# A fused diffusion-backbone step: routing weight at eviction, expert pairs summed by the gather, outputs accumulated onto rows that hold the bias

## What is computed

```
def _layer_norm(x, g, b):
    y = (x - mean(x)) * rsqrt(var(x) + LN_EPS)
    return y * g + b

def _hier_moe(u, ...):
    p_group = softmax(u @ w_r1 + b_r1);  g_val, g_idx = top_k(p_group, 1)
    e_val, e_idx = top_k(fine logits of that group, 2)
    e_w = softmax(e_val) * g_val                  # two weights per token
    y = sum over the 2 experts of e_w * (silu(a) * b) @ w_down   # a, b = u @ w_up[expert]

x = _layer_norm(ALPHA * x + gate2 * _hier_moe(u2), ln2_g, ln2_b)
```

## Time and profile before

| | |
|---|---|
| runs of the kernel before | 1146.58, 1149.21, 1150.54 us (median 1149.21) |
| the profiled execution | 1147.15 us, of which the span is 1145.3 us |
| busy share of the span | PE 88%, PE weight loads 66%, DVE 54%, ACT 38%, POOL 15% |
| mean granted TensorE clock | 0.939 of 2.4 GHz |
| chain that ended last | PE 77%, DVE 12%, DMA 5%, ACT 3% |

### The profile page before, as it was taken

The page is one execution under the profiler, slowest core; times in us unless marked ns, Lnnn a source line. Parts: engine busy times, 40 slices in busy tenths (PEclk is TensorE's granted clock), DMA queues, the critical chain, the costliest instruction groups (busy, mean ns, idle before and its releaser), DMA issues.

```text
span 1145.3 us, 13287 instructions
## 1 busy us (share of the span) xinstructions
PE 1004.3 (88%) x4607; PEld 758.4 (66%) x4607; DVE 621.7 (54%) x897; ACT 438.1 (38%) x603; POOL 174.0 (15%) x139
## 2 busy tenths in 40 slices
PE   5899899998999999989998995389999999999800
PEld 1113799985777777766666774378888888888700
DVE  0176641100453455640317856676889965799548
ACT  0001422213343434421205002165787854788422
POOL 2035023000000000000000734111101101010056
PEclk9999999999999999999999896599999999999965
DMA  9995722204020302261207006487799997699552
GB/s 323 394 353 209 282 75 74 74 0 164 20 74 1 111 1 74 22 210 45 73 1 275 19 37 220 163 301 289 277 398 400 398 359 275 225 399 400 191 214 92
DMA packets 90747, 215.04 MB, mean 188 GB/s; under 512 B 6538, under 2 KB 7744, under 8 KB 90704
## 3 DMA queue, kind: packets, MB, share of 16 engines
q1 hardware_dynamic: 73904, 165.86, 40.1%
q10 hardware_dynamic: 11108, 30.07, 7.2%
q0 software_dynamic: 5696, 18.58, 4.6%
HBM read 191.37 MB, written 23.12 MB: 187 GB/s over the span
## 4 chain that ended last, share of the span: by engine, by line
PE 77%; DVE 12%; DMA 5%; ACT 3%; issue 2%; SPq 1%; ACTq 0%; POOL 0%; POOLq 0%; DVEq 0%
PE ps L1734 27%; PE ps L1521 22%; PE ps L1440 10%; PE ps L1507 7%; DMA ring<-in_w_mod 3%; PE ps L1625 2%; PE ps L1726 1%; PE ps L1492 1%; PE ps L1564 1%; DVE R_x L991 1%; DMA out<-small 1%; ACT w_hi L695 1%; PE ps L1619 1%; PE ps L1614 1%; PE ps L1761 1%
## 5 line engine op out<-in xcount | busy, mean ns | idle before, releaser
L1521 PE MATMUL ps<-w_hi,uT_hi 128*128 128x512 f32 x320 | 132.9, 415 | 7.2 <-ACT R_x L773 2.5
L1052 DVE TENSOR_TENSOR w_lo<-ring,w_hi 128x1024 fp32r<-128x1024 f32 x52 | 62.3, 1223 | 128.3 <-ACT w_hi L695 127.0
L1521 PE MATMUL ps<-w_lo,uT_hi 128*128 128x512 f32 x320 | 126.3, 395 | 0.0
L1440 PE MATMUL ps<-ring,small 128*2 128x512 f32 x192 | 87.6, 618 | 13.1 <-DMA ring<-in_w_mod 12.8
L1251 DVE TENSOR_TENSOR wa_lo<-ring,wa_hi 128x1024 fp32r<-128x1024 f32 x64 | 74.1, 1219 | 4.4 <-ACT wa_hi L851 4.0
L1521 PEld LDWEIGHTS ps<-w_hi,uT_hi 128*128 128x128 f32 x320 | 60.6, 189 | 23.7 <-issue 4.0
L1440 PEld LDWEIGHTS ps<-ring,small 128*2 128x2 f32 x192 | 16.5, 87 | 83.4 <-issue 82.2
L615 POOL TENSOR_TENSOR R_u<-R_m 128x1024 f32<-128x1024 f32 x1 | 2.4, 2397 | 449.6 <-DVE R_m L1218 449.6
L1521 PEld LDWEIGHTS ps<-w_lo,uT_hi 128*128 128x128 f32 x320 | 60.7, 190 | 13.4
L1734 PE MATMUL ps<-wa_hi,xgT_hi 128*128 128x512 f32 x152 | 62.9, 414 | 5.2 <-DVE xgT_lo L1358 5.2
L1521 PE MATMUL ps<-w_hi,uT_lo_a 128*128 128x512 f32 x160 | 64.0, 400 | 0.0
(11 more groups left out here) (345 smaller groups left out, 2238.1 us busy)
## 6 DMA issues: line engine op xcount, KB each, us to landing
ring<-in_w_up SPq DMA_DIRECT2D x64, 512.0 KB, 8.7
ring<-in_w_mod SPq DMA_DIRECT2D x12, 2048.0 KB, 18.0
ring<-in_w_in SPq DMA_DIRECT2D x11, 2048.0 KB, 7.9
R_d<-in_w_up SPq DMA_DIRECT2D x32, 512.0 KB, 10.9
R_p<-in_w_down SPq DMA_DIRECT2D x32, 512.0 KB
R_h<-in_w_down SPq DMA_DIRECT2D x32, 512.0 KB
y_slots<-R_m ACTq DMA_DIRECT2D x19, 512.0 KB, 6.3
R_s<-in_w_up SPq DMA_DIRECT2D x16, 512.0 KB
```

The source lines that it names most:

```text
L1052: tt(lo[:, at], weights(name)[:, at], hi[:, at].bitcast(F32), ALU.subtract).then_inc(S["w_split"], 1)
L1440: i = mm(out, lhs(k), rhs(k), start=(k == 0), stop=(k == n - 1))
L1521: i = mm(out, parts(k)[a][:, tok(j)], w[b][:, k], start=(k == 0 and a + b == 0), stop=(k == KD - 1 and b == 1))
```

## The change

Four edits. First, the weight of every slot is worked out in the routing: `hot_tile` times the token number goes to a table of its own (`hot_tok`), `hot_tile` times the weight stays in its place, and PE multiplies that with `hot_place` too (a second product, "wslot", into bank 0). DVE copies the result to `w_slot`. ACT's eviction copies the tile's column to `w_now` and scales by it, so that the stored rows are weighted already. Second, the gathers: both choices of block 0 and the first choices of blocks 1 to 4 are plain; the second choices of blocks 1 to 4 add themselves to the rows of the first (`compute_op=ALU.add`), each issued after its first choice has landed. ACT's scaling and DVE's weighted sum go away; DVE adds plainly for block 0. Third, `finish` now does (x - mean) * g2 over the whole block in one DVE instruction, and ACT multiplies by one over the deviation. Fourth, POOL writes `ln2_b` to all output rows near the start (five DMAs of 512 KB, DRAM to DRAM), and at the end it issues the five output stores as accumulating DMAs onto these rows. POOL's and DVE's products with `g2` and sums with `b2` go away.

```diff
@@ routing, DVE and PE
-                i = tt(hot, hot, const("tok").rearrange("p (j a) -> p j a", a=1).to_broadcast([P, NT, MAXT]), ALU.mult)
+                i = tt(hot_tok[:, s_ * NT:(s_ + 1) * NT], hot, const("tok").rearrange("p (j a) -> p j a", a=1).to_broadcast([P, NT, MAXT]), ALU.mult)
...
-            tt(w12[:, 1], w12[:, 0], route_b, ALU.mult).then_inc(S["weights_ready"], 1)
+            ch(tt(w12[:, 1], w12[:, 0], route_b, ALU.mult))
+            for s_ in range(2):
+                hot = hot_tile[:, s_ * NT:(s_ + 1) * NT]
+                tt(hot, hot, w12[:, s_].rearrange("p (j a) -> p j a", a=1).to_broadcast([P, NT, MAXT]), ALU.mult).then_inc(S["wslots_hot"], 1)
             take(dve, "slots")
             release(nc.vector.tensor_copy(tile_idx[:], bank(1)[:, 0:MAXT]), "slots")
+            take(dve, "wslot")
+            release(nc.vector.tensor_copy(w_slot, bank(0)[:, 0:MAXT]), "wslot")
...
+            pe.wait_ge(S["wslots_hot"], 2)
+            begin(pe, "wslot")
+            for n_ in range(2 * NT):
+                i = mm(bank(0)[:, 0:MAXT], hot_place[:, n_], hot_tile[:, n_], start=(n_ == 0), stop=(n_ == 2 * NT - 1))
+            filled(i, "wslot")
@@ SP, before the third piece of the first down weights
-                        sp.wait_ge(S["weights_ready"], 1)
+                        take(sp, "wslot")
                         sp.wait_ge(S["gathered"], 16)
@@ ACT, evict
+                nc.scalar.copy(w_now, w_slot[:, bass.ds(s, 1)]).then_inc(S["w_now"], 1)
                 act.wait_ge(S["down_full"], 2 * s + 1)
                 act.wait_ge(S["y_stored"], 16 * s + 1)
-                nc.scalar.copy(y_sb[:, 0:BW], bank(2)).then_inc(S["y_ready"], 1)
+                act.wait_ge(S["w_now"], s + 1)
+                nc.scalar.activation(y_sb[:, 0:BW], bank(2), ACT.Copy, scale=w_now).then_inc(S["y_ready"], 1)
                 act.wait_ge(S["down_full"], 2 * s + 2)
-                nc.scalar.copy(y_sb[:, BW:D], bank(3)).then_inc(S["y_ready"], 1)
+                nc.scalar.activation(y_sb[:, BW:D], bank(3), ACT.Copy, scale=w_now).then_inc(S["y_ready"], 1)
@@ POOL, start (between the loads of w_r and of b_r)
+            for j in range(NT):
+                pool.dma_start(out_rows(j), ln2_b[0].partition_broadcast(P)).then_inc(b2_stored[j], 16)
@@ POOL, end
-            for j in range(NT):
-                for s in range(2):
-                    nc.gpsimd.indirect_dma_start(out=y_pair[j][:, s], out_offset=None, in_=y_slots,
...
-            for j in range(NT - 1):
-                pool.wait_ge(S["f_norm"], j + 1)
-                chain(nc_t(x_tok[:, j], x_tok[:, j], ROW2["g2"], ALU.mult))
-                nc_t(x_tok[:, j], x_tok[:, j], ROW2["b2"], ALU.add).then_inc(S["f_ready"], 1)
+            gather_slots(0, 0, y_pair[0][:, 0], ALU.bypass)
+            gather_slots(0, 1, y_pair[0][:, 1], ALU.bypass)
+            for j in range(1, NT):
+                gather_slots(j, 0, y_pair[j][:, 0], ALU.bypass)
+            for j in range(1, NT):
+                pool.wait_ge(pair_loaded[j], 16)
+                gather_slots(j, 1, y_pair[j][:, 0], ALU.add)
+            for j in range(NT):
+                pool.wait_ge(S["f_norm"], j + 1)
+                pool.wait_ge(b2_stored[j], 16)
+                pool.dma_start(out_rows(j), x_tok[:, j], accum_op=ALU.add).then_inc(S["out_stored"], 16)
+            pool.wait_ge(S["out_stored"], 16 * NT)
@@ ACT, end: scale_first, the bias of line 947 and the stores of lines 952 and 954 go
-                nc.scalar.activation(x_tok[:, j], x_tok[:, j], ACT.Identity, bias=shift_mean[:, j:j + 1],
-                                     scale=rstd[:, j:j + 1]).then_inc(S["f_norm"], 1)
+                nc.scalar.mul(x_tok[:, j], x_tok[:, j], rstd[:, j:j + 1]).then_inc(S["f_norm"], 1)
@@ DVE, end
-                stt(shift_mean[:, j:j + 1], mv[:, 2 * j:2 * j + 1], -1.0, rstd[:, j:j + 1], ALU.mult, ALU.mult).then_inc(S["f_pre"], 1)
+                stt(x_tok[:, j], x_tok[:, j], mv[:, 2 * j:2 * j + 1], ROW2["g2"], ALU.subtract, ALU.mult).then_inc(S["f_pre"], 1)
...
-                dve.wait_ge(S["y1_scaled"], j + 1)
-                ch(stt(yp[:, 0], yp[:, 1], w12[:, 1, j:j + 1], yp[:, 0], ALU.mult, ALU.add))
+                if j == 0:
+                    ch(tt(yp[:, 0], yp[:, 0], yp[:, 1], ALU.add))
...
-            ch(tt(x_tok[:, jl], x_tok[:, jl], ROW2["g2"], ALU.mult))
-            tt(x_tok[:, jl], x_tok[:, jl], ROW2["b2"], ALU.add).then_inc(S["f_ready_last"], 1)
```

More of the change, by code:

```diff
@@ L169, in plan_psum @@
     fill("slots", "b1")
+    fill("wslot", "b0")
     return fills
@@ L349, in backbone @@
         prod = rt(NT, EPG, NG)
+        hot_tok = R_h[:, rt_at[0]:rt_at[0] + 2 * NT * MAXT].rearrange("p (n t) -> p n t", n=2 * NT)
         e1, e2, both, rank, prod16 = (rt(NT, NE) for _ in range(5))
@@ L380, in backbone @@
         w12 = cols(10).rearrange("p (s j) -> p s j", s=2)
+        w_slot = cols(MAXT)
+        w_now = cols(1)
         pool_scratch = cols(1)
@@ L409, in backbone @@
             "vec_loaded", "up_hi", "down_hi", "up_split", "down_split", "w_hi_done", "w_split", "w_hi_free", "uT_ready", "wg_split", "mT_hi_ready", "proj_loaded", "hidT_lo_ready", "xgT_lo_ready", "wg_loaded", "weights_ready", "wpool_loaded",
-            "wr_loaded", "x1_pre", "x1_ready", "x_back", "x_loaded", "x_loaded1", "x_ready", "x_spilled", "xgT_full",
+            "wslots_hot", "w_now", "wr_loaded", "x1_pre", "x1_ready", "x_back", "x_loaded", "x_loaded1", "x_ready", "x_spilled", "xgT_full",
             "xgT_ready", "xn_ready", "y_ready", "y_stored", "ya_ready", "zeros_stored")}
+        b2_stored = [sem(f"b2_stored_{j}") for j in range(NT)]
         pair_loaded = [sem(f"pair_loaded_{j}") for j in range(NT)]
@@ L483, in piece_sem, with out_rows @@
             return piece_loaded[4 * i + q]
+        def out_rows(j):
+            return y_prompt[0] if j == 0 else y_sample[0, (j - 1) * P:j * P, :]
         def seg(s):
@@ L646, in _, with gather_slots @@
             pool.wait_ge(S["experts_done"], 1)
-            for j in range(NT):
-                for s in range(2):
-                    nc.gpsimd.indirect_dma_start(out=y_pair[j][:, s], out_offset=None, in_=y_slots,
-                                                 in_offset=bass.IndirectOffsetOnAxis(ap=slot_idx[:, s * NT + j:s * NT + j + 1], axis=0)
-                                                 ).then_inc(pair_loaded[j], 16)
-            for j in range(NT - 1):
+            def gather_slots(j, s, dst, op):
+                nc.gpsimd.indirect_dma_start(out=dst, out_offset=None, in_=y_slots,
+                                             in_offset=bass.IndirectOffsetOnAxis(ap=slot_idx[:, s * NT + j:s * NT + j + 1], axis=0),
+                                             compute_op=op).then_inc(pair_loaded[j], 16)
+            gather_slots(0, 0, y_pair[0][:, 0], ALU.bypass)
[5 more added lines that the diff above has]
+                gather_slots(j, 1, y_pair[j][:, 0], ALU.add)
+            for j in range(NT):
                 pool.wait_ge(S["f_norm"], j + 1)
-                chain(nc_t(x_tok[:, j], x_tok[:, j], ROW2["g2"], ALU.mult))
-                nc_t(x_tok[:, j], x_tok[:, j], ROW2["b2"], ALU.add).then_inc(S["f_ready"], 1)
+                pool.wait_ge(b2_stored[j], 16)
+                pool.dma_start(out_rows(j), x_tok[:, j], accum_op=ALU.add).then_inc(S["out_stored"], 16)
+            pool.wait_ge(S["out_stored"], 16 * NT)
         @block.scalar
@@ L933, in _ @@
             nc.scalar.copy(scratch1[0:1, 3:4], const("one")[0:1, :]).then_inc(S["experts_done"], 1)
[L935 to L940, removed]
             for j in range(NT):
-                if j + 1 < NT:
-                    scale_first(j + 1)
                 act.wait_ge(S["f_var"], j + 1)
@@ L1349, in _ @@
             ch(tt(w12[:, 0], m1, g_val, ALU.mult))
-            tt(w12[:, 1], w12[:, 0], route_b, ALU.mult).then_inc(S["weights_ready"], 1)
+            ch(tt(w12[:, 1], w12[:, 0], route_b, ALU.mult))
+            for s_ in range(2):
+                hot = hot_tile[:, s_ * NT:(s_ + 1) * NT]
+                tt(hot, hot, w12[:, s_].rearrange("p (j a) -> p j a", a=1).to_broadcast([P, NT, MAXT]),
+                   ALU.mult).then_inc(S["wslots_hot"], 1)
             take(dve, "slots")
             release(nc.vector.tensor_copy(tile_idx[:], bank(1)[:, 0:MAXT]), "slots")
+            take(dve, "wslot")
+            release(nc.vector.tensor_copy(w_slot, bank(0)[:, 0:MAXT]), "wslot")
             nc.vector.memset(scratch1[0:1, 2:3], 0.0).then_inc(S["y_stored"], 1)
@@ L1716, in _ @@
                 pe.wait_ge(S["onehots"], 2 + n_ + 1)
-                i = mm(bank(1)[:, 0:MAXT], hot_place[:, n_], hot_tile[:, n_], start=(n_ == 0), stop=(n_ == 2 * NT - 1))
+                i = mm(bank(1)[:, 0:MAXT], hot_place[:, n_], hot_tok[:, n_], start=(n_ == 0), stop=(n_ == 2 * NT - 1))
             filled(i, "slots")
-            for n_ in ("rank", "slots", ("uT2", NT - 1, 0), ("uT2", NT - 1, 1), ("out", 4), ("out", 3)):
```

(3 more changed lines are left out.)

9 lines of the change are left out of this document (removed).

## The result

The changed kernel takes 1156.13 us (median of 8 runs, 1153.95 to 1160.2) against 1147.58 for the kernel before (median of 8): ratio 1.0077, 95% interval 1.0063 to 1.0092. The profiled execution after has a span of 1155.6, before 1145.3: 10.3 us to find.

A forecast was written before the change was run, and what follows sets the result against it. It took PE to bound the experts and DVE the end; end -4.7, routing -0.8, experts 0 and start +0.5 gave -5.0 on the profiled 1147.15, so 1144.2 us by the runs' median, range 1140.5 to 1152.3.

The forecast's parts named there:

- 6.6 of slack: Start: the last `w_mod` load lands at 92.4 and is needed at 99.02, leaving 6.6 us.
- +0.5: Start: cost in us taken for the five b2 DMAs, as part of their bytes goes beside the loads.
- bound of +2.3: Start: largest cost in us, if all b2 bytes (8.9 us) go ahead of the last `w_mod` load.
- 0.4 to the end: End: time in us from the last store's landing to the span's end, taken as before the change.
- term of -0.65: End, behind the last block's variance: 7.6 us instead of 8.26, with the adding store landing in 4.14.
- +1.8: End, block 1: the gate's product starts at 1110.9 instead of 1109.13, waiting for the first adding pair, landed at 1109.46.
- POOL is held up: Rival, end: the first add's issue costs 1.75 us more beside DVE's work; time 1146.0, no change; chance 0.11.
- -5.85: End, blocks 2 to 4: 5.95 us per block instead of 7.90, three times.
- -0.8: Routing: POOL issues the gather at about 730.8 instead of 731.91, so `xgT_lo` comes at 739.4 instead of 740.22.
- the prices eat the gain: Rival: p near 4.96, no routing gain, half the start's cost; time 1150.6, no change; chance 0.21.
- p: End: time an adding DMA takes for 512 KB, taken as 2.48 us, between 1.24 and 4.96.
- Evictions make PE wait: Rival, experts: ACT's detour exceeds `xgT_lo`'s 0.5 us in some 17 tiles; at 0.7 us time 1156.1, slower; chance 0.05.

The follow-up runs named there:

- alone: The kernel before with only the five b2 stores added where the change has them: ratio 1.0052, 6.0 us.
- taken away: The changed kernel with its five b2 stores issued behind the pooled stage instead of between the router's loads: ratio 1.0028, 5.6 us better than the change.
- the two kernels with a wait added: The kernel before with POOL also waiting at its end, once for ACT's five output stores (1.0049), once for DVE's last pass (1.0016).
- The run with plain pairs: The changed kernel with b2 stores behind the pooled stage and all ten end gathers plain, DVE adding every pair, accumulating output stores kept: ratio 1.0036.
- What paid, without what cost: The changed kernel without b2 and accumulating stores; POOL adds b2 to blocks 0 to 3, DVE finishes the last, adding gathers for blocks 2 to 4: 1144.0 us, 0.9972.

## Why the prediction was wrong

Three terms of its sum failed, and the sum's sign with them.

- **"6.6 of slack" at the start.** The bytes were priced well: the load issued at 64.4 and 64.8 took 8.2 longer to land (17.1 before, 25.3 after), the two behind it 9.8 longer, near the 8.9 that the prediction named if all went first. The choice of +0.5, with part of the bytes beside the loads, did not hold. What failed with it is the slack, which was read off the last load alone. The load issued at 64.4 landed at 81.5. PE wanted it at 85.35 in the change, whose trace stands 0.4 later there, so its slack was 3.5, and it was the first to run out: 8.2 - 3.5 = 4.7, near the wait of 4.83. The bound of +2.3 fell with that. The low clock behind a wait (1.4) was not in the sum at all. Measured: +6 (alone +6.0, taken away -5.6).
- **"0.4 to the end".** The prediction took over the gap behind ACT's store for a program that POOL leaves last. "POOL has no more work behind its waits than these issues, and nobody waits for POOL but the end" was right, and the end was just what waited: 5.05 behind POOL's last wait by the two kernels with a wait added. No row of before showed this, as it lay 0.3 us under the end that ACT's landing set. With the store's landing of 5.2 instead of 4.14, the term of -0.65 became +5.8.
- **The first adding pair, "+1.8".** The time of an adding transfer was close: 199 GB/s make 2.6 of 512 KB (taken: 2.48), and the four landed at 1117.6, 1120.0, 1122.6 and 1125.1. The first one was issued well before the sixth gather landed, as forecast. What failed is the step "moves behind those still under way": it let the pair land 2.48 behind the sixth gather, and the pair landed 4.65 behind it (1117.61 against 1112.96), 9.1 after its issue. So the gate came 3.5 late. How much of this is the issue, which took 2.43 instead of 0.94, was not separated. The rival "POOL is held up" named part of that issue: in the change and five experiments an adding gather took 1.54 to 1.57 to issue with none of DVE's passes over two 128x1024 operands beside it, and 2.0 to 2.6 with one.

What was right: the length of the periods of blocks 2 to 4, so -5.4 of the -5.85 (5.95 forecast, 5.96 and 5.97, once 6.35; there DVE's reciprocal started 0.4 later behind ACT's root, with its pair landed 3.9 before, and why is not shown); the routing (-1.2 for -0.8, with POOL's copy and issue as foreseen), some of it lost again at the first tile; the experts at 0. With the measured sizes in the forecast's own sum: +6.6 at the start, -1.2 + 0.8 at routing and first tile, +3.5 - 5.4 + 5.8 at the end give +10.1 of the 10.3 us by which the profiles differ.

The size of the periods' gain was right, but the reading of the period before was not complete. The prediction put what lies between variance and gate down to the work of "the pair's sum and the two small instructions behind it". DVE's and POOL's timeline before shows that 2.1 of it were DVE's wait beside POOL's passes:

```profile
1107.54 1.28 DVE L1418 SCALAR_TENSOR_TENSOR ring<-ring,small 128x1024 f32<-128x1024 f32 x1
...
1109.06 0.16 DVE L1413 SCALAR_TENSOR_TENSOR small<-small 128x1 f32<-128x1 f32 x1
...
1113.31 1.59 DVE L1418 SCALAR_TENSOR_TENSOR ring<-ring,small 128x1024 f32<-128x1024 f32 x1
...
1113.89 3.20 POOL L657 TENSOR_TENSOR R_x<-R_x,ring 128x1024 f32<-128x1024 f32 x1
...
1115.13 1.98 DVE L1413 SCALAR_TENSOR_TENSOR small<-small 128x1 f32<-128x1 f32 x1
...
1121.20 1.59 DVE L1418 SCALAR_TENSOR_TENSOR ring<-ring,small 128x1024 f32<-128x1024 f32 x1
```

The first two rows have no pass of POOL beside them. A block later the same two instructions take 1.59 and 1.98 instead of 1.28 and 0.16, and the small one ends 0.02 behind POOL's pass. From the first pair sum to the second it takes 5.77, from the second to the third 7.89. So the periods became shorter because POOL's passes with `g2` and `b2` left the end. The pair sum that went (1.28) made room for (x - mean) * g2 on DVE (1.28), no more. The run with plain pairs shows it from the other side: all pair sums stay, DVE has that pass on top, POOL has none, and the periods are 6.80 instead of 7.90. No run takes POOL's passes away alone.

The rivals: "the prices eat the gain" named the right direction but put most of it on p, which was as forecast. The end and the start failed by latencies and slack instead. "Evictions make PE wait" has 1156.1, the measured time, but by chance: from 780 to 1085 PE is busy 305.00 of 305 us. Of the prediction's signs of being wrong one came, an issue on POOL above 1.5 us; for POOL's way out of the program it named none.

One point stays open: where ACT waits in POOL's place, the span ended 2.9 behind the landing and 7.3 behind the end of POOL's last issue. Whether POOL's way out starts only when its issued transfer is written out was not tried. Why the DMA engines moved 295 instead of 387 GB/s beside the b2 stores was not separated either.

## What to carry to other kernels

Before moving the last store to another engine, ask when that engine leaves the program: here POOL had to be through 5 us before the end. Without the b2 stores and the adding output stores, with short work on POOL in the middle and the last block on DVE and ACT's queue, a loss of 8.6 us became a gain of 7.6. Slack in a stream of loads is that of the tightest load in the stream, not of the last one, so new traffic belongs where no load is awaited. An adding gather paid here only where its first half had landed early: gather those first halves early, and give the blocks that are needed first plain pairs. Before a pass is taken off the engine that bounds a stage, look whether one of its small instructions is long: here 0.16 became 1.98, which was a wait beside POOL's pass, and moving that pass was the gain.

## What the runs showed of the hardware that was not expected

- POOL's way out of the program: 5.05 us from its last wait (5.2 to 5.9 where that wait was for a store of its own), beside 0.4 to 0.5 where ACT, SP and DVE wait for the same store.
- In the changed kernel an adding gather took 1.54 to 2.43 to issue instead of 0.94, landed 8.8 to 10.1 after its issue (plain ones 4.3 to 6.2), and the DMA engines moved 199 GB/s with such gathers under way. In "What paid, without what cost" the last one, issued 4.9 behind the one before, landed after 6.1. An output store of 512 KB landed 2.6 behind its issue by ACT's queue, 3.0 by POOL's, and 5.1 to 7.0 where it adds onto DRAM.
- A DVE pass with two SBUF operands that starts during a POOL pass ends only behind it: 3.15 and 1.6 instead of 1.28 and 1.22 (in the kernel before 1.59 and, for 128x1, 1.98 instead of 1.28 and 0.16), and 1.29 where it starts 0.02 behind POOL's end. The Trainium skill's page "SBUF — State Buffer" (SBUF: two separate sides) describes the shared port pair as an exclusive lock that whichever of the two starts first keeps for its whole instruction; the traces agree.
